# RWKV-7 stage of a three-model kernel: the vector products of a step in another order, and the bonus sum and two transposes moved in TensorE's queue

## What is computed

```python
def wkv7_step(state, inp):
    r, w, k, v, a, b = inp
    sa = jnp.einsum('...ij,...j->...i', state, a)
    state = (state * w[..., None, :] + sa[..., :, None] * b[..., None, :]
             + v[..., :, None] * k[..., None, :])
    y = jnp.einsum('...ij,...j->...i', state, r)
    return state, y

def rwkv7_bidir_branch(p, mu, w0, w2, a0, a2, k_k, k_a, r_k, lnx_g, lnx_b):
    ...
    decay = jnp.exp(-jnp.exp(-jax.nn.softplus(-z_w) - 0.5))
    a = jax.nn.sigmoid(a0[:, None, None, :] + jnp.einsum('dbsl,dlc->dbsc', ad, a2))
    kk = heads(k * k_k)
    kk = kk * lax.rsqrt(jnp.maximum(jnp.sum(kk * kk, axis=-1, keepdims=True), 1e-12))
    k = k * (1.0 + (a - 1.0) * k_a)
    ...
    xs = (to_scan(r), to_scan(decay), to_scan(k), to_scan(v), to_scan(-kk), to_scan(kk * a))
    _, y = lax.scan(wkv7_step, init, xs)
    ...
    out = layer_norm(y_sum, ...)
    bonus = jnp.sum(r * k * r_k, axis=-1, keepdims=True) * v
    out = out + bonus[0] + bonus[1]
```

## Time and profile before

| what | value |
|---|---|
| time of the profiled execution | 5210.79 us |
| its span, first to last instruction | 5209.0 us |
| median of three timed runs | 5210.79 us |
| PE busy over the span | 4575.4 us (88%) |
| DVE busy | 2522.9 us (48%) |
| ACT busy | 1594.9 us (31%) |
| POOL busy | 478.8 us (9%) |
| stretch of the 16 steps | 4237 to 5097 us |

### The profile page before, as it was taken

One profiled execution on the slowest core, in us unless ns is written; L12 is line 12 of the kernel. 1 busy time (PEld: TensorE's weight loads), 2 busy tenths in 40 slices (PEclk: granted clock), 3 DMA queues, 4 the chain that ended last, 5 costly groups with the idle time before them and its releaser, 6 DMA issues. The chain is left out here.

```text
span 5209.0 us, 80602 instructions
## 1 busy us (share of the span) xinstructions
PE 4575.4 (88%) x31952; PEld 3361.8 (65%) x31952; DVE 2522.9 (48%) x3966; ACT 1594.9 (31%) x2447; POOL 478.8 (9%) x447
## 2 busy tenths in 40 slices
PE   8888999998899989999997896878897889898987
PEld 7655787663578757888886642356665347666675
DVE  3633533422253341788887389644424135454552
ACT  2322321311232131666665200032212123333432
POOL 0110000000000000233223000000000012212120
PEclk9877999996699999999999998989998999999997
DMA  3201222221022232111111311111222110000001
GB/s 149 82 17 53 87 87 101 81 81 49 25 85 84 101 121 92 58 47 57 53 53 40 117 65 65 51 63 65 81 81 81 68 63 34 19 19 19 19 19 65
DMA packets 36922, 338.01 MB, mean 65 GB/s; under 512 B 4112, under 2 KB 6416, under 8 KB 18832
## 3 DMA queue, kind: packets, MB, share of 16 engines
q1 hardware_dynamic: 36624, 333.80, 17.7%
HBM read 321.20 MB, written 12.58 MB: 64 GB/s over the span
## 5 line engine op out<-in xcount | busy, mean ns | idle before, releaser
L515 PE MATMUL ps<-hi,weight_parts 128*128 128x512 f32 x5056 | 1601.8, 398 | 178.6 <-DVE lo L391 76.8
L515 PEld LDWEIGHTS ps<-hi,weight_parts 128*128 128x128 f32 x5056 | 973.5, 193 | 400.4 <-issue 169.1
L515 PE MATMUL ps<-lo,weight_parts 128*128 128x512 f32 x2528 | 1002.6, 397 | 0.0
L502 DVE TENSOR_TENSOR weight_parts<-w,weight_parts 128x1024 fp32r<-128x1024 f32 (+1 forms) x320 | 387.2, 1211 | 999.9 <-ACT weight_parts L492 999.8
L492 ACT ACTIVATE weight_parts<-w 128x1024 fp32r<-128x1024 f32 (+1 forms) x320 | 335.0, 1048 | 1238.7 <-PE ps L515 1074.0
L515 PEld LDWEIGHTS ps<-lo,weight_parts 128*128 128x128 f32 x2528 | 487.8, 193 | 102.0
L3056 PEld LDWEIGHTS ps<-buffers 64*64 64x64 f32 x12544 | 433.5, 136 | 145.5 <-issue 143.1
L3056 PE MATMUL ps<-buffers 64*64 64x64 f32 x12544 | 463.7, 226 | 70.7 <-issue 45.4
L2643 PE MATMUL ps<-x,w 128*128 128x512 f32 x768 | 343.4, 610 | 60.9 <-DVE buffers L2679 33.5
L2188 PE MATMUL ps<-x_parts,column_parts 128*128 128x512 f32 x1536 | 364.9, 395 | 9.9 <-DVE column_parts L2414 9.9
L2188 PEld LDWEIGHTS ps<-x_parts,column_parts 128*128 128x128 f32 x1536 | 287.7, 189 | 75.0 <-DVE column_parts L2414 10.4
(11 more groups left out here) (484 smaller groups left out, 5750.2 us busy)
## 6 DMA issues: line engine op xcount, KB each, us to landing
w<-in_weights SPq DMA_DIRECT2D x126, 2048.0 KB, 8.0
w<-in_wh SPq DMA_DIRECT2D x64, 512.0 KB, 3.9
v_kept<-buffers SPq DMA_DIRECT2D x4, 1024.0 KB, 5.3
buffers<-v_kept SPq DMA_DIRECT2D x16, 256.0 KB, 2.6
h<-x_kept SPq DMA_DIRECT2D x2, 2048.0 KB, 7.8
x<-in_xT SPq DMA_DIRECT2D x4, 512.0 KB, 11.5
x_kept<-h SPq DMA_DIRECT2D x1, 2048.0 KB, 8.7
vc_kept<-x SPq DMA_DIRECT2D x4, 512.0 KB, 2.6
```

What stands on the lines that cost most here:

```text
L502: dve.tensor_tensor(K.parts[:, j % 2, 1, 0:nk, :], K.W[:, slot, :].rearrange("p (k n) -> p k n", k=8)[:, 0:nk, j * P:(j + 1) * P], K.parts ...
L515: mm = pe.matmul(ps, K.parts[:, j % 2, m, k, :], x[:, k * T:(k + 1) * T], start=(first and k == 0 and n == 0), stop=(last and k == nk - 1 ...
```

## The change

Three things move inside a step, and one PSUM bank changes.

- DVE: after `kk` come `ahat` and `rhat` (now behind the wait for ACT's `ee`), then `b`, `bhat`, `a1`, `kp`, `khat` and last `rk`. `rk` is written over RQ and not over LW. `bo2` stands directly behind `bo`, ahead of `upd(p, pd, 1)`.
- PE: `bon` moves ahead of `ch_sa(p, pd, 1)` and of `tv`, directly behind the second projection, with its wait for `rk`. `tb` moves behind `ch_ys(p, pd, 1)` and waits for `bo2` in place of `bhat`; `tk` follows directly. `tb` goes to bank 5, the bank of `bon`, in place of bank 1.
- Waits that are no longer there: PE's for `bhat`, `khat`, `bt` and `rhat`, and POOL's for `bo2` ahead of the levels. `aa` is now waited for at `sa`.

No operation is added or removed.

```diff
@@ pool
                 pool.wait_ge(AM.sem, AM.count(n, "as"))
-                pool.wait_ge(DM.sem, DM.count(n, "bo2"))
@@ tensor
                 if n is not None:
                     projection(1)
+                if n is not None:
+                    pe.wait_ge(DM.sem, DM.count(n, "rk"))
+                    if fin is not None:
+                        pe.wait_ge(K.sem("fin_act"), K.count("fin_act", 3 * fin[0] + 2))
+                    pe.matmul(K.ps[:, 5, :], same, RQ, start=True, stop=True).then_inc(PM.step("bon"), 1)
                 ch_sa(p, pd, 1)
...
                     mm.then_inc(PM.step("tv"), 1)
-                    pe.wait_ge(AM.sem, AM.count(n, "aa"))
-                    pe.wait_ge(DM.sem, DM.count(n, "bhat"))
-                    K.apart(pe)
-                    for j in range(8):
-                        mm = heads(K.ps[:, 1, 64 * j:64 * j + 64], BK[:, 0, 64 * j:64 * j + 64], one)
-                    mm.then_inc(PM.step("tb"), 1)
-                    pe.wait_ge(DM.sem, DM.count(n, "rk"))
-                    ...
-                    pe.matmul(K.ps[:, 5, :], same, LW, start=True, stop=True).then_inc(PM.step("bon"), 1)
                 ch_ys(p, pd, 1)
                 if n is not None:
+                    pe.wait_ge(DM.sem, DM.count(n, "bo2"))
+                    K.apart(pe)
+                    for j in range(8):
+                        mm = heads(K.ps[:, 5, 64 * j:64 * j + 64], BK[:, 0, 64 * j:64 * j + 64], one)
+                    mm.then_inc(PM.step("tb"), 1)
                     pe.wait_ge(AM.sem, AM.count(n, "vt"))
-                    pe.wait_ge(DM.sem, DM.count(n, "khat"))
...
-                    pe.wait_ge(AM.sem, AM.count(n, "bt"))
-                    pe.wait_ge(DM.sem, DM.count(n, "rhat"))
+                    pe.wait_ge(AM.sem, AM.count(n, "aa"))
...
-                    pe.wait_ge(DM.sem, DM.count(n, "bo2"))
@@ scalar
-                    ... (("vt", "tv", VT, 4), ("bt", "tb", BT, 1), ("kt", "tk", KT, 4)):
+                    ... (("vt", "tv", VT, 4), ("bt", "tb", BT, 5), ("kt", "tk", KT, 4)):
@@ vector
                     dve.scalar_tensor_tensor(RN, KQ, cv("k_k", c), RN, ALU.mult, ALU.mult).then_inc(DM.step("kk"), 1)
+                    dve.wait_ge(AM.sem, AM.count(n, "ee"))
                     dve.wait_ge(DM.sem, DM.count(n, "kk"))
+                    dve.scalar_tensor_tensor(AR[:, d, :, 0, :], chunks(RN), -1.0, chunks(EP), ALU.mult, ALU.mult)\
+                       .then_inc(DM.step("ahat"), 1)
+                    dve.tensor_tensor(AR[:, d, :, 1, :], chunks(RQ), chunks(L), ALU.mult).then_inc(DM.step("rhat"), 1)
                     dve.tensor_tensor(LW, RN, AA, ALU.mult).then_inc(DM.step("b"), 1)
-                    dve.wait_ge(AM.sem, AM.count(n, "en"))
...
                     dve.wait_ge(DM.sem, DM.count(n, "kp"))
-                    dve.scalar_tensor_tensor(LW, RQ, cv("r_k", c), KQ, ALU.mult, ALU.mult).then_inc(DM.step("rk"), 1)
-                    dve.wait_ge(AM.sem, AM.count(n, "ee"))
-                    ... ahat
                     dve.tensor_tensor(BK[:, 1, :], KQ, EN, ALU.mult).then_inc(DM.step("khat"), 1)
-                    ... rhat
+                    dve.scalar_tensor_tensor(RQ, RQ, cv("r_k", c), KQ, ALU.mult, ALU.mult).then_inc(DM.step("rk"), 1)
                     dve.wait_ge(PM.sem, PM.count(n, "bon"))
...  (bo, and now bo2 directly behind it)
                 upd(p, pd, 1)
-                ... bo2
```

More of the change, by code:

```diff
@@ L2974, in wkv @@
     levels = range(1, 6)
-    PM = Marks(K, "wkv_pe", "wa kkn tv tb bon tk sa srb sk " +
+    PM = Marks(K, "wkv_pe", "wa kkn bon tv tb tk sa srb sk " +
                " ".join(f"t{l}a t{l}b ct{l}a ct{l}b" + (f" cx{l}a cx{l}b" if l < 5 else "") for l in levels))
     AM = Marks(K, "wkv_act", "sw aa sqk ln rn ep en eplus ee vt bt kt as " + " ".join(f"t{l}a t{l}b" for l in levels))
-    DM = Marks(K, "wkv_dve", "r k v lw scan lprev max kk b bhat a1 kp rk ahat khat rhat bo bo2 xt0 x0 mrb mak mrk " +
+    DM = Marks(K, "wkv_dve", "r k v lw scan lprev max kk ahat rhat b bhat a1 kp khat rk bo bo2 xt0 x0 mrb mak mrk " +
                " ".join(f"xt{l}a xt{l}b" + (f" x{l}a x{l}b" if l < 5 else "") for l in levels))
@@ L3151, in step @@
                     mm.then_inc(PM.step("tv"), 1)
-                    pe.wait_ge(AM.sem, AM.count(n, "aa"))
-                    pe.wait_ge(DM.sem, DM.count(n, "bhat"))
+                ch_ys(p, pd, 1)
+                if n is not None:
+                    pe.wait_ge(DM.sem, DM.count(n, "bo2"))
                     K.apart(pe)
                     for j in range(8):
-                        mm = heads(K.ps[:, 1, 64 * j:64 * j + 64], BK[:, 0, 64 * j:64 * j + 64], one)
+                        mm = heads(K.ps[:, 5, 64 * j:64 * j + 64], BK[:, 0, 64 * j:64 * j + 64], one)
                     mm.then_inc(PM.step("tb"), 1)
-                    pe.wait_ge(DM.sem, DM.count(n, "rk"))
-                    if fin is not None:
-                        pe.wait_ge(K.sem("fin_act"), K.count("fin_act", 3 * fin[0] + 2))
-                    pe.matmul(K.ps[:, 5, :], same, LW, start=True, stop=True).then_inc(PM.step("bon"), 1)
-                ch_ys(p, pd, 1)
-                if n is not None:
                     pe.wait_ge(AM.sem, AM.count(n, "vt"))
-                    pe.wait_ge(DM.sem, DM.count(n, "khat"))
                     K.apart(pe)
@@ L3301, in step @@
                 if n is not None:
-                    for name, src, dst, bank in (("vt", "tv", VT, 4), ("bt", "tb", BT, 1), ("kt", "tk", KT, 4)):
+                    for name, src, dst, bank in (("vt", "tv", VT, 4), ("bt", "tb", BT, 5), ("kt", "tk", KT, 4)):
                         act.wait_ge(PM.sem, PM.count(n, src))
@@ L3390, in step @@
                     dve.wait_ge(DM.sem, DM.count(n, "kp"))
-                    dve.scalar_tensor_tensor(LW, RQ, cv("r_k", c), KQ, ALU.mult, ALU.mult).then_inc(DM.step("rk"), 1)
-                    dve.wait_ge(AM.sem, AM.count(n, "ee"))
-                    dve.scalar_tensor_tensor(AR[:, d, :, 0, :], chunks(RN), -1.0, chunks(EP), ALU.mult, ALU.mult)\
-                       .then_inc(DM.step("ahat"), 1)
                     dve.tensor_tensor(BK[:, 1, :], KQ, EN, ALU.mult).then_inc(DM.step("khat"), 1)
-                    dve.tensor_tensor(AR[:, d, :, 1, :], chunks(RQ), chunks(L), ALU.mult).then_inc(DM.step("rhat"), 1)
+                    dve.scalar_tensor_tensor(RQ, RQ, cv("r_k", c), KQ, ALU.mult, ALU.mult).then_inc(DM.step("rk"), 1)
                     dve.wait_ge(PM.sem, PM.count(n, "bon"))
@@ L3399, in step @@
                         dve.tensor_tensor(BO[:, par, :], K.ps[:, 5, :], VQ, ALU.mult).then_inc(DM.step("bo"), 1)
+                        dve.tensor_copy(TMP[:, 0:64], VQ[:, 0:64]).then_inc(DM.step("bo2"), 1)
                     else:
                         dve.tensor_tensor(TMP, K.ps[:, 5, :], VQ, ALU.mult).then_inc(DM.step("bo"), 1)
[L3402 to L3406, removed]
                         dve.wait_ge(DM.sem, DM.count(n, "bo"))
                         dve.tensor_tensor(BO[:, par, :], BO[:, par, :], TMP, ALU.add).then_inc(DM.step("bo2"), 1)
+                upd(p, pd, 1)
                 gk(p, pd, 2)
```

## The result

The changed kernel takes 5257.27 us (median of four runs, 5252.36 to 5262.55), the kernel before 5207.8 us (four runs, 5204.52 to 5211.51). The ratio is 1.0095, with a 95% interval of 1.0078 to 1.0112: slower by nearly one per cent, 49.5 us by the medians.

What follows compares the result with a forecast made beforehand. PE's queue was taken as the bound in the 16 steps. Waits of 39.5 us, plus 5 and 8 for the clock, minus 6.5 for code, gave 46 us on 5210.8: about 5256 us, range 5234 to 5276.

Steps and rivals of the forecast that it cites:

- The head of the queue and the chain on DVE: At `bon`, PE waits for `rk`, which ends 5.17 us behind `ee`: 4.1 us for middle d = 1, 0.85 for d = 0.
- DVE's wait for `bon` with d = 0: Sign in the d = 0 steps: this wait shrinks from 3.0 us to about 1.1.
- PE waiting for `rk`: Sign in the waits view: some 30 to 40 us of PE waiting, in 16 pieces.
- Steps 14 and 15: Last steps, no projections as cover: +4.75 and +3.3 us of waiting, plus 2.5 us of low clock each.
- Steps 0 and 1: First steps, without `finish`, counted like d = 0: 0.85 us of waiting each, a lower bound for step 0.
- Middle steps with d = 0: No `finish` ahead of ACT's exponentials, so `ee` is earlier: 0.85 us of PE waiting at `bon` in each.
- Middle steps with d = 1: Six steps, n = 3 to 13: 24.6 us waiting at `bon`, 8 us low clock, 6.5 us of code gaps regained.
- the stop under the weight load: PE's 1.92 us code gap in step 7 falls partly into the `rk` wait: 1.1 us a step regained, -6.5 us.
- The wait of `tb` for `bo2`: New PE wait behind `ch_ys(1)`: taken as 0, bounds 0 and 0.3 us a step.
- the clock up to `sa`: Middle d = 1 steps: clock falls in about half, 8 us in all; bounds 0 and 3.4 us a step.
- the clock falls in every step: Rival: clock falls in every step with the long wait, 5272 us, chance 0.17.
- Much given back: Rival: waits fall together with code gaps and the clock holds, 24 us slower, 5235 us, chance 0.12.

Runs made afterwards that it cites:

- The halves of the change: Two kernels: only PE's new order with DVE's old one, 5222.1 us (ratio 1.0025); only DVE's new order with PE's old one, 5223.99 us (1.0026).
- tv_first: Changed kernel with `bon` one place later, behind `ch_sa(1)` and `tv`: 5251.69 us, ratio 1.0078 to the kernel before.
- fill_small_load: Changed kernel with four extra products ahead of the `rk` wait in six middle d = 1 steps and weight loads cut to 64 columns: 5254.09 us, ratio 1.0086.
- after_small_load: Changed kernel with each of eight weight loads cut from 4096 to 64 columns a partition: 5254.04 us, ratio 1.0090 to the kernel before.
- fill_wait: Changed kernel with four extra 512-column products ahead of the `rk` wait in the six middle d = 1 steps: 5263.69 us, ratio 1.0097 to the kernel before.

## Why the forecast held, step by step

- The head of the queue and the chain on DVE: right. `ahat` starts right behind `ee`, `rk` 4.39 us behind it (4.38 forecast), and PE waits 4.21 us for d = 1 with `finish` (4.1) and 0.90 us for d = 0 (0.85). The halves of the change confirm the arithmetic of the cover: 1.07 us are left where `rk` is early. Of the signs that were named, DVE's wait for `bon` with d = 0 shrank from 3.0 us to 1.45 (1.1 forecast), and one was off: 51.9 us of PE waiting for `rk` instead of 30 to 40, because in steps 14 and 15 PE stands at `bon` for 7.00 and 10.54 us; the forecast had only their net cost, 4.75 and 3.3 us.
- Steps 14 and 15: +8.05 us of waiting and +5 us of clock were forecast, 13 us. Step 14 is 6.8 us longer, and in step 15 the copy of `sa` comes 6.0 us later, from its `lw`: 12.8 us.
- Steps 0 and 1: 1.7 us forecast, 6.1 measured, the one group of steps for which too little was forecast. The prediction said that step 0 was a lower bound: it has no recurrence work ahead, so PE stood at `bon` for 3.0 us instead of 0.85, and the clock fell there too.
- Middle steps with d = 0: 5.1 us forecast, 3.1 measured.
- Middle steps with d = 1: 24.6 of waiting, 8 of clock and 6.5 given back, so 26 us, were forecast; the six steps are 19.9 us longer. Up to the copy of `sa` they are 36 us later (4.2 us of wait and some 1.9 us of low clock in each), and 16 us of that come back behind it. Both last terms were mis-sized, and against each other. The clock fell in all six, not in half of them (0.67 to 0.78 from `bon` to the copy of `sa`): to that extent the rule of the Trainium skill (TensorE: Matmul & The Clock Gate, Part 1: The HAM clock gate) was the better guide, and the trace agrees with it. But the price that the prediction's upper bound put on it, 3.4 us a step, did not arrive: it was 1.9 us up to `sa`, and taking it away (with the loads cut) brought the copy of `sa` forward by 10.9 us and shortened the six steps by 2.3. What came back was 16 us and not 6.5. About 10 us of it are the stop under the weight load; 1.1 us a step were taken for it, within bounds of 0 and 1.9. Another 2.5 us come from the end of steps 5 and 9, where a round of the loop ends: PE stands there for 5.0 and 4.9 us before and for 4.0 and 3.5 us in the changed kernel, a stop that the prediction did not look at. The rest is shorter stops of PE elsewhere behind `sa`.
- The wait of `tb` for `bo2`, costed at 0 to 0.3 us a step: right in the changed kernel, and tight, as `tv_first` shows.

The sum came out at 46 us against 49.5 by the medians and 42.4 between the two traces. Four terms were off by 2 to 10 us each, partly against each other: steps 0 and 1 (4.4 too small), the middle steps with d = 0 (2.0 too large), the clock up to `sa` (3.7 too small) and what comes back (9.9 too small). The sign and the size rest on the waits; the closeness is partly luck. Shifting the borders moves the time of either kernel by more than 20 us. That the difference stays at 47 us under that shift is the evidence that the forecast did not hang on it.

The rival "the clock falls in every step" had its mechanism right and its time wrong. "Much given back" had its mechanism in part: 16 us came back in the middle d = 1 steps, but the clock took some of it first.

What stays open: how the low clock and the late code make up for each other. The traces of `fill_small_load` and after_small_load show that what the full clock gains up to `sa` turns into longer stops of PE behind it (6.9 of 8.6 us). That an engine at half speed asks for its next block later, so that the block is late by less, would do it, but which packet is late for which reason was not followed. `fill_wait` and `fill_small_load` also have 16 more instructions in each of the six steps and so other borders.

## What to carry to other kernels

A result that comes off a second engine belongs behind the work of the first that needs nothing from it; before moving it forward, write down when it will be there (the chain from its last outside input, here the end of `ee` plus 5.2 us) and when the queue will ask for it. Two halves that each cost a quarter of a per cent can cost one per cent together, because each was the other's cover. And where a queue is dense with small instructions, look at its unexplained gaps: moving a large load by half a step and shifting the code by 32 instructions gained 34 to 39 us here, where the wrong order lost 49.

## What was not expected of the hardware

- 32 idle semaphore increments in each step with a projection made a 5.2 ms kernel 21 us faster (0.9957, 0.9943 to 0.9970), as far as shown by moving gaps of the small products to the wide ones. The Trainium skill says that the cost of crossing from one instruction block to the next is mostly hidden (Runtime: NRT & Kernel Launch, Instruction fetch mechanics). In this stage the traces do not agree: 49.9 us of unexplained waits became 18.6 by shifting the code.
- Eight weight loads of 2 MB made PE stand still with nothing waited for and cost 9 to 10.5 us, which went when the loads were moved under a stretch of wide products. That the load makes PE's code late is the reading of it; no run shows the delay of a packet itself.
- A wait of 4.2 us, not far behind eight wide products at full rate, was followed by a fall of the clock in all six steps (0.50 in the window of step 7), and keeping the clock up by filling the wait brought no gain in the time that is clear of noise.
